# A hybrid decoder step on one core: all cache copies on the load queue, ten value slots, later splits of the output weights

## The chip, the cores and the metric

The kernel runs on one NeuronCore of a Trainium2 chip. The time is the device time of one execution in microseconds (us). The kernel before was timed in three runs: 383.45 us median, 382.65 to 383.95. One further execution was profiled; its own time was 379.59 us, with a span of 377.5 us between its first and its last instruction. PE is TensorE, DVE VectorE, ACT ScalarE, POOL GpSimd and SP SyncE.

## The reference

One layer step for a prompt of 512 tokens and a sample of 8 sequences with 8 new tokens each (64 rows), model width 1024. All values are float32.

- One input projection `w_in` (1024 x 4096) gives q, k, v and a gate for 8 attention heads of 64, and b, c, h and a gate for 512 channels of a short convolution.
- Attention: three causal branches per head, (window, dilation) = (128, 1), (512, 4), (2048, 16), merged by their softmax denominators, which is one softmax over the union of keys with each key weighted by how many branches hold it. The sample also looks at a cache of 2048 past keys and values per sequence; of these 1280 are ever looked at.
- Convolution: `u = c * h`, `y = causal 3-tap convolution of u` (with a state of two rows for the sample), `z = b * y * silu(g_conv)`.
- `mix = [attention * silu(g_att), z]`, one output projection `w_out` (1024 x 1024), then `LayerNorm(2**0.25 * x + out)` with gain and bias.
- Outputs: the new rows of x, and the new key and value caches and convolution states. The caches are returned as a whole, so the old keys and values (67 MB) are copied from inputs to outputs.

## The kernel before

**Numbers.** To keep float32 accuracy on TensorE each operand is split into a high part (a float32r cast by ScalarE) and a low part (what is left, a subtraction by VectorE), and each product is three matmuls: high by high, high by low, low by high. `x_hi`/`x_lo` hold the activations, `w_hi`/`w_lo` two weight tiles, `wo` both parts of `w_out`.

**Input projection.** `w_in` comes as 32 tiles of 128 output features (`w_tiles`, 512 KB each). A tile is loaded into one of two slots of `w_raw` (`load_w`, L227), cast (`split_hi`, L396, the cast is L402), subtracted (`split_lo`, L678, L681) and used by `project` (L1001, matmuls L997 to L999), in two halves of 288 token columns, `pj[0]` and `pj[1]`. A load of tile t waits until tile t-2 has been subtracted; a cast of tile t waits until tile t-2 has been projected.

**Rounds.** After three first tiles (v, q, k of head pair 0) the kernel runs over four head pairs: three rounds of eight tiles (`pe_round` L1156, `act_round` L556, `dve_round` L853) and a last, shorter one (`pe_last_round` L1209, `act_last_round` L605, `dve_last_round` L894). A round projects c, h, b and the convolution's gate, the next pair's v, this pair's attention gate, and the next pair's q and k, and weaves in the pair's attention for the prompt (`prompt_scores`, `prompt_turn`, `prompt_values`) and for the sample (`sample_scores` over four key pieces, `sample_turn`, `sample_values` over ten value pieces). The order on every engine is written out by hand; semaphores tie them together.

**Cache pieces.** Of each head pair's cache the used part comes as 4 key pieces (1280 KB each, one slot each in `k_buf`) and 10 value pieces (512 KB each), for which `v_buf` has 8 slots (`V_SLOTS`, L45). `load_v` (L241) waits until the piece that held its slot has been used (L1139 counts). So eight pieces of the next round can be loaded as soon as this round's are used, while pieces 8 and 9 come within their round.

**Queues.** All loads and the stores of new values are issued by SyncE, in the order of its program (L249 to L358). All copies of the caches from DRAM to DRAM, 60 of 1 MB or 1.25 MB, are issued by ScalarE: `copy_next()` (L434) stands between its other instructions, 12 times in each round. First go 24 pieces of the unused rest, then 16 of the used keys, then 20 of the used values. SyncE's program in a round:

```python
for j in range(5):
    load_w(t0 + 3 + j)
    if j:
        load_k(i + 1, j - 1)
    if i == 0 and j < 4:
        load_v(0, 2 * j); load_v(0, 2 * j + 1)
load_w(t0 + 8); load_w(t0 + 9)
load_v(i, 8); load_v(i, 9); save_v(i + 1)
load_v(i + 1, 0); load_v(i + 1, 1)
load_w(t0 + 10)
for n in range(2, 8): load_v(i + 1, n)
save_k(i + 1)
```

**Output projection.** The eight pieces of `w_out` are loaded in the last round (`load_wo`, L307), into space that the attention's buffers give free; `split_wo` (L538, cast L540) and `split_wo_lo` (L794, L797) make their two parts. TensorE multiplies five token tiles (0, 1, 2, the sample, 3; L1256 to L1300), VectorE adds the residual and does the LayerNorm (L954 to L989), SyncE loads the residual rows (`x_res`) and stores `y`. Before the first matmul (L1294) the first parts of `mix` must be split (`split_mix` L543, `split_mix_lo` L800); on VectorE that stands behind all eight `split_wo_lo`.

**Convolution and gates.** `conv_taps` (L780) makes `y_pad`, `conv_out_half` (L824) multiplies it by b into `zb`, `gate_half` (L759) makes 1 / (1 + exp(-g)) and multiplies. `out_sample` (L527) copies the sample's attention out of PSUM into `o_s`, `sample_out_turn` (L1149) transposes it at the start of the next round.

## Time and profile before

| | |
|---|---|
| three timed runs | 383.45 us median (382.65 to 383.95) |
| profiled execution, own time | 379.59 us |
| its span | 377.5 us |
| mean granted TensorE clock | 0.989 |
| PE busy | 353.8 us, 94% |
| DVE, ACT, POOL busy | 198.5 us, 117.4 us, 10.9 us |
| DMA | 141.06 MB, mean 374 GB/s |
| queue of SyncE (q1), of ScalarE (q10) | 73.46 MB, 67.11 MB |

Times are counted from the first instruction. A row of a timeline is one instruction or a run of equal ones: start, duration, engine, line, operation, tiles written and read, and in brackets how long the engine was idle before it and what ended that. SPq and ACTq are instructions that issue a DMA. A row of windows gives a stretch, its length, the busy time and count of instructions for PE, its weight loads, DVE, ACT and POOL, then the granted clock (1.00 is 2.4 GHz), the busy share of the 16 DMA engines and what they moved.

### The profile page before, as it was taken

To read this page: it belongs to the slowest core of one execution; us is meant where nothing else is said; L and a number is where in the kernel's file an instruction comes from. 1 tells how busy PE (TensorE), PEld (TensorE's weight loads), DVE (VectorE), ACT (ScalarE), POOL (GpSimd) and SP (SyncE) were. 2 spreads that over 40 slices of the span, in tenths; PEclk is the share of its full clock that TensorE was granted. 3 is DMA by queue.
4 is the path that set the end of the run, shared out by engine and by line. 5 is a ranking of instruction groups with operands and counts; after the bars stand their busy time and mean duration, and the time that the engine had idled before them with its cause. 6 is when DMAs were issued, how large, how long until landed. Compare 5 with 4: busy or idle time off the path is not lost.

```text
span 377.5 us, 7664 instructions
## 1 busy us (share of the span) xinstructions
PE 353.8 (94%) x3256; PEld 311.3 (82%) x3256; DVE 198.5 (53%) x371; ACT 117.4 (31%) x236; POOL 10.9 (3%) x28
## 2 busy tenths in 40 slices
PE   1999999997999999999999799999998998999991
PEld 1899888896988888999988689999787997888780
DVE  2533446817314368571242486711536799284765
ACT  4523423313213243431241243412525643220100
POOL 0010000000000000001000000010000002000000
PEclk9999999998999999999999999999999999999997
DMA  7999999999999999899999999999999886999931
GB/s 279 408 413 423 419 417 423 419 423 422 413 416 418 421 379 413 316 403 369 394 418 418 383 418 395 423 394 406 415 416 408 326 333 216 366 317 366 361 124 56
DMA packets 34547, 141.06 MB, mean 374 GB/s; under 512 B 3409, under 2 KB 3793, under 8 KB 32465
## 3 DMA queue, kind: packets, MB, share of 16 engines
q1 hardware_dynamic: 18194, 73.46, 48.9%
q10 hardware_dynamic: 16320, 67.11, 45.8%
q8 instruction: 26, 0.43, 0.4%
q14 instruction: 7, 0.06, 0.0%
HBM read 135.80 MB, written 71.86 MB: 550 GB/s over the span
## 4 chain that ended last, share of the span: by engine, by line
PE 62%; DMA 28%; DVE 4%; ACT 2%; SPq 2%; issue 1%; ACTq 0%
DMA w_raw<-in_w_tiles 26%; PE pj_a L997 7%; PE pj_b L997 6%; PE pj_a L999 6%; PE pj_a L998 6%; PE pj_b L998 6%; PE pj_b L999 6%; PE sc L1136 5%; PE px L1294 3%; PE px L1296 3%; PE px L1295 3%; PE sc L1100 2%; DVE w_lo L681 2%; ACT w_hi L402 2%; DMA k_buf<-in_xT 2%; PE po L1079 1%
## 5 line engine op out<-in xcount | busy, mean ns | idle before, releaser
L997 PE MATMUL pj_a<-x_hi,w_hi 128*128 128x288 f32 x256 | 79.8, 312 | 9.7 <-DVE x_lo L688 8.3
L997 PE MATMUL pj_b<-x_hi,w_hi 128*128 128x288 f32 x256 | 79.1, 309 | 0.0
L998 PE MATMUL pj_a<-x_lo,w_hi 128*128 128x288 f32 x256 | 76.5, 299 | 0.0
L999 PE MATMUL pj_a<-x_hi,w_lo 128*128 128x288 f32 x256 | 76.5, 299 | 0.0
L998 PE MATMUL pj_b<-x_lo,w_hi 128*128 128x288 f32 x256 | 76.1, 297 | 0.0
L999 PE MATMUL pj_b<-x_hi,w_lo 128*128 128x288 f32 x256 | 75.9, 297 | 0.0
L681 DVE TENSOR_TENSOR w_lo<-w_raw,w_hi 128x1024 fp32r<-128x1024 f32 x32 | 39.1, 1223 | 50.9 <-ACT w_hi L402 50.9
L997 PEld LDWEIGHTS pj_a<-x_hi,w_hi 128*128 128x128 f32 x256 | 49.2, 192 | 18.3 <-issue 9.3
L402 ACT CAST w_hi<-w_raw 128x1024 fp32r<-128x1024 f32 x32 | 33.5, 1046 | 87.3 <-DMA w_raw<-in_w_tiles 55.6
L997 PEld LDWEIGHTS pj_b<-x_hi,w_hi 128*128 128x128 f32 x256 | 48.6, 190 | 4.1 <-issue 2.6
L998 PEld LDWEIGHTS pj_a<-x_lo,w_hi 128*128 128x128 f32 x256 | 49.3, 193 | 0.0
L999 PEld LDWEIGHTS pj_a<-x_hi,w_lo 128*128 128x128 f32 x256 | 49.2, 192 | 0.0
L998 PEld LDWEIGHTS pj_b<-x_lo,w_hi 128*128 128x128 f32 x256 | 48.6, 190 | 0.0
L999 PEld LDWEIGHTS pj_b<-x_hi,w_lo 128*128 128x128 f32 x256 | 48.5, 190 | 0.0
L767 DVE RECIPROCAL rg<-rg 128x288 f32<-128x288 f32 x16 | 31.2, 1953 | 0.6
L488 ACT ACTIVATE p_pr<-p_pr,stat 128x512 f32<-128x512 f32 (+3 forms) x32 | 17.7, 555 | 27.1 <-DVE stat L732 27.1
L732 DVE CUSTOM_DVE_ANT_0 p_pr<-px,mask_pr 128x512 f32<-128x512 f32 (+3 forms) x32 | 14.4, 486 | 18.8 <-PE px L1049 18.8
L1136 PE MATMUL sc<-v_buf,pt_s 128*32 128x128 f32 x640 | 21.4, 276 | 0.0
L1100 PE MATMUL sc<-k_buf,q_bd 128*32 128x320 f32 x256 | 20.5, 438 | 0.9 <-DVE stat L754 0.9
L1294 PE MATMUL px<-wo,x_hi 128*128 128x512 f32 x48 | 19.1, 397 | 1.2 <-issue 1.2
L1296 PE MATMUL px<-wo,x_lo 128*128 128x512 f32 x48 | 19.0, 396 | 0.0
L1136 PEld LDWEIGHTS sc<-v_buf,pt_s 128*32 128x32 f32 x640 | 16.3, 109 | 3.3 <-issue 3.0
(124 smaller groups left out, 403.4 us busy)
## 6 DMA issues: line engine op xcount, KB each, us to landing
k_buf<-in_k_used SPq DMA_DIRECT2D x16, 1280.0 KB, 15.2
v_buf<-in_v_used SPq DMA_DIRECT2D x40, 512.0 KB, 18.4
out_k_used_out<-in_k_used ACTq DMA_DIRECT2D x16, 1280.0 KB, 11.6
out_v_used_out<-in_v_used ACTq DMA_DIRECT2D x20, 1024.0 KB, 10.8
w_raw<-in_w_tiles SPq DMA_DIRECT2D x32, 512.0 KB, 11.5
out_k_rest_out<-in_k_rest ACTq DMA_DIRECT2D x12, 1024.0 KB, 11.5
out_v_rest_out<-in_v_rest ACTq DMA_DIRECT2D x12, 1024.0 KB, 11.3
wo_raw<-in_w_out SPq DMA_DIRECT2D x8, 512.0 KB, 8.6
```

The costliest lines, as they stand in the source:

```text
L402: nc.scalar.copy(w_hi[:, c], w_raw[:, c]).then_inc(w_hi_done, 1)
L488: nc.scalar.activation(p, p, ACT.Exp, bias=negmax_pr[:, e:e + 1], scale=-1.0, accum_out=sum_pr[:, e:e + 1]).then_inc(pr_exp, 1)
L681: nc.vector.tensor_tensor(w_lo[:, c], w_raw[:, c], w_hi[:, c].bitcast(F32), ALU.subtract)\
L732: nc.vector.tensor_tensor_reduce(out=p_pr[:, e * SEQ:e * SEQ + w], in0=px[e][:, 0:w], in1=mask_pr[:, SEQ - w:], scale=-SCALE, scalar=BIG, ...
L767: nc.vector.reciprocal(rg[:, c], rg[:, c]).then_inc(g_step, 1)
L997: nc.tensor.matmul(out, w_hi[:, w], x_hi[:, c], start=(k == 0), stop=False)
L998: nc.tensor.matmul(out, w_hi[:, w], x_lo[:, c], start=False, stop=False)
L999: return nc.tensor.matmul(out, w_lo[:, w], x_hi[:, c], start=False, stop=(k == KT - 1))
L1100: last = nc.tensor.matmul(sc[r * 32:r * 32 + 32, 0:K_COLS], q, k_buf[:, k0:k0 + K_COLS], start=(b == 0), stop=(b == 1 and not ends), skip_ ...
L1136: last = nc.tensor.matmul(sc[r * 32:r * 32 + 32, b * P:(b + 1) * P], pt_s[:, t * P + r * 32:t * P + r * 32 + 32], v_buf[:, v0:v0 + P], sta ...
L1294: nc.tensor.matmul(out, x_hi[:, tok], wo[:, hi], start=(n == 0), stop=False)
L1296: last = nc.tensor.matmul(out, x_lo[:, tok], wo[:, hi], start=False, stop=(n == KT - 1))
```

## The change

- The copies leave ScalarE. `copy_next()` and its helpers stand in SyncE's program, on the queue of the loads; the order of the 60 copies is the same. In the loop each step is a weight tile's load, then value or key pieces, then one or two copies: 11 copies a round. Four stand in the start, eight in the last round beside the loads of `w_out`, two behind the last two weight tiles, and 13 among the loads of `x_res` and the stores of `y`.
- `V_SLOTS` is 10. The value pieces of a head pair are loaded in their own round, behind its first four weight tiles; the last round's behind its two weight tiles and between the pieces of `w_out`.
- Room for the two slots: `zb` goes, `conv_out_half` writes its product back into `y_pad`; `o_s` is now the first 256 columns of `y_pad`. So the first tap waits on `so_turned`, and the gate's multiply of the second half becomes one of 224 prompt columns and one of 64 sample columns.
- In the last round `split_wo(0)`, `(1)` and `(2)` move behind the moves of the sample's turns (`move_sample`), with the subtractions `split_wo_lo(0)` to `(2)` later too.

```diff
-V_SLOTS = 8
+V_SLOTS = V_PIECES
...
-        zb = sb("zb", [P, NT])
-        o_s = sb("o_s", [P, 2 * P], stack=early)
+        o_s = y_pad[:, 0:2 * P]
...
             load_k(0, 1)
+            copy_next()
             save_v(0)
             load_w(5)
             load_k(0, 2)
+            copy_next()
             load_k(0, 3)
+            copy_next()
+            copy_next()
             save_k(0)
             for i in range(NPAIR - 1):
                 t0 = tile0(i)
...
+                load_w(t0 + 3)
+                for n in range(0, 3):
+                    load_v(i, n)
+                copy_next()
+                load_w(t0 + 4)
+                for n in range(3, 6):
+                    load_v(i, n)
+                copy_next()
+                load_w(t0 + 5)
+                for n in range(6, 8):
+                    load_v(i, n)
+                copy_next()
+                copy_next()
+                load_w(t0 + 6)
+                for n in range(8, 10):
+                    load_v(i, n)
+                copy_next()
+                copy_next()
+                load_w(t0 + 7)
+                load_k(i + 1, 0)
+                copy_next()
+                load_w(t0 + 8)
+                load_k(i + 1, 1)
+                copy_next()
+                load_w(t0 + 9)
+                load_k(i + 1, 2)
+                copy_next()
+                save_v(i + 1)
+                load_w(t0 + 10)
+                load_k(i + 1, 3)
+                copy_next()
+                copy_next()
+                save_k(i + 1)
             load_w(W_TILES - 2)
+            for n in range(0, 2):
+                load_v(NPAIR - 1, n)
+            copy_next()
             load_w(W_TILES - 1)
+            for n in range(2, 4):
+                load_v(NPAIR - 1, n)
+            copy_next()
...
             sp.wait_ge(k_used, pieces + 1)
             load_wo(0)
+            load_v(NPAIR - 1, 4)
+            load_v(NPAIR - 1, 5)
+            copy_next()
             sp.wait_ge(k_used, pieces + 2)
             load_wo(1)
+            load_v(NPAIR - 1, 6)
+            load_v(NPAIR - 1, 7)
+            copy_next()
             sp.wait_ge(k_used, pieces + 3)
             load_wo(2)
+            load_v(NPAIR - 1, 8)
+            load_v(NPAIR - 1, 9)
+            copy_next()
+            copy_next()
             sp.wait_ge(k_used, pieces + 4)
             load_wo(3)
             load_wo(4)
+            copy_next()
...
             load_wo(5)
             load_wo(6)
+            copy_next()
+            copy_next()
             sp.wait_ge(s_masked, K_PIECES * NPAIR)
             load_wo(7)
-            load_v(NPAIR - 1, 8)
-            load_v(NPAIR - 1, 9)
+            copy_next()
...
                              d["x_rows"][y_rows(t), :]).then_inc(res_in[t % 2], 16)
+                for _ in range((0, 4, 4, 3, 2)[t]):
+                    copy_next()
...
                 exp_prompt(i, 3)
-                copy_next()
-                split_wo(0)
                 exp_sample(i)
                 move_prompt(i, 3)
                 split_hi(t0 + 4)
-                copy_next()
-                split_wo(1)
                 out_prompt(i)
                 move_sample(i, 0)
                 move_sample(i, 1)
-                split_wo(2)
+                split_wo(0)
+                split_wo(1)
                 exp_gate(t0 + G_CONV, 0)
                 move_sample(i, 2)
+                split_wo(2)
                 split_wo(3)
...
-                if gate == 0:
-                    nc.vector.tensor_tensor(rg[:, c], rg[:, c], zb[:, c], ALU.mult).then_inc(g_step, 1)
+                if gate == 0 and h == 0:
+                    nc.vector.tensor_tensor(rg[:, c], rg[:, c], y_pad[:, c], ALU.mult).then_inc(g_step, 1)
+                elif gate == 0:
+                    nc.vector.tensor_tensor(rg[:, HALF:SEQ], rg[:, HALF:SEQ], y_pad[:, HALF:SEQ], ALU.mult)\
+                        .then_inc(g_prompt, 1)
+                    r = rg[:, SEQ:].rearrange("p (b t) -> p b t", t=DEC_SEQ)
+                    nc.vector.tensor_tensor(r, r, y_s[:, :, 0:DEC_SEQ], ALU.mult).then_inc(g_step, 1)
+                    dve.wait_ge(g_prompt, i + 1)
...
                     dve.wait_ge(padded, i + 1)
+                    if i:
+                        dve.wait_ge(so_turned, i)
...
                 conv_taps(i, 1)
-                split_wo_lo(0)
                 norm_sample(i)
                 conv_taps(i, 2)
                 conv_out_half(i, 0)
                 conv_out_half(i, 1)
                 split_lo(t0 + 4)
+                split_wo_lo(0)
                 split_wo_lo(1)
-                split_wo_lo(2)
                 z_read(i)
                 gate_half(i, 0, 0)
+                split_wo_lo(2)
                 split_wo_lo(3)
                 gate_half(i, 0, 1)
```

## Rows read from the trace of the kernel before

**Rows 1.** Windows by stage: stretch, its length, each engine's busy time, clock, DMA share, GB/s.
```profile
31.30:109.10 77.80, 75.72 (x758) 67.67 (x756) 38.23 (x78) 24.02 (x50) 1.24 (x5) 0.98 1.02 419
109.10:183.40 74.30, 74.30 (x762) 66.55 (x758) 37.31 (x77) 23.74 (x52) 2.29 (x5) 1.00 0.99 391
183.40:260.00 76.60, 74.42 (x762) 66.64 (x758) 37.21 (x77) 23.79 (x52) 2.29 (x5) 1.00 1.01 405
260.00:314.90 54.90, 53.18 (x601) 46.47 (x599) 35.68 (x72) 26.09 (x53) 0.38 (x2) 1.00 0.94 370
314.90:316.70 1.80, 0.61 (x20) 0.36 (x17) 1.80 (x3) 0.37 (x1) 0.00 (x0) 1.00 0.02 5
```

**Rows 2.** Waits, whole span: total us, times, longest.
```profile
ACT w_hi L402 <- DMA w_raw<-in_w_tiles: 55.6, 12, 11.2
```

**Rows 3.** Timeline of ScalarE, three casts of weight tiles: start, us; idle time before.
```profile
83.90 1.05 ACT L402 CAST w_hi<-w_raw 128x1024 fp32r<-128x1024 f32 x1 [7.67 <-DMA w_raw<-in_w_tiles]
...
210.99 1.05 ACT L402 CAST w_hi<-w_raw 128x1024 fp32r<-128x1024 f32 x1 [11.18 <-DMA w_raw<-in_w_tiles]
...
284.48 1.04 ACT L402 CAST w_hi<-w_raw 128x1024 fp32r<-128x1024 f32 x1 [4.12 <-DMA w_raw<-in_w_tiles]
```

**Rows 4.** Timeline of SyncE's queue at the end of the second round.
```profile
175.53 0.33 SPq L231 DMA_DIRECT2D w_raw<-in_w_tiles  x1
175.90 7.43 SPq L246 DMA_DIRECT2D v_buf<-in_v_used  x6
...
185.69 1.35 SPq L231 DMA_DIRECT2D w_raw<-in_w_tiles  x1
```

**Rows 5.** DMA queue of the page: packets, MB, share of 16 engines' span.
```profile
q10 hardware_dynamic: 16320, 67.11, 45.8%
```

**Rows 6.** Windows around two stalls: before, in and behind the first, then the third round's.
```profile
82.50:85.90 3.40, 3.40 (x26) 3.17 (x24) 0.92 (x1) 2.00 (x4) 0.00 (x0) 1.00 1.01 415
85.90:89.30 3.40, 1.56 (x36) 1.09 (x35) 3.30 (x5) 1.61 (x4) 0.00 (x0) 1.00 1.01 413
89.30:92.70 3.40, 3.15 (x13) 3.18 (x14) 3.30 (x6) 0.00 (x0) 0.00 (x0) 0.51 1.04 433
...
208.00:214.60 6.60, 4.42 (x41) 3.90 (x39) 2.53 (x5) 1.80 (x3) 0.00 (x0) 1.00 0.97 382
```

**Rows 7.** DMA issues of the page: KB each, median us to landing.
```profile
k_buf<-in_k_used SPq DMA_DIRECT2D x16, 1280.0 KB, 15.2
v_buf<-in_v_used SPq DMA_DIRECT2D x40, 512.0 KB, 18.4
out_k_used_out<-in_k_used ACTq DMA_DIRECT2D x16, 1280.0 KB, 11.6
out_v_used_out<-in_v_used ACTq DMA_DIRECT2D x20, 1024.0 KB, 10.8
w_raw<-in_w_tiles SPq DMA_DIRECT2D x32, 512.0 KB, 11.5
```

**Rows 8.** Windows by what the DMA engines move.
```profile
245.00:246.50 1.50, 1.50 (x36) 1.14 (x35) 0.46 (x1) 0.40 (x1) 0.00 (x0) 1.00 0.99 410
...
330.00:337.00 7.00, 7.00 (x31) 5.63 (x31) 6.63 (x11) 2.38 (x3) 0.00 (x0) 1.00 1.03 317
...
225.00:262.00 37.00, 37.00 (x427) 34.44 (x418) 18.60 (x27) 11.29 (x21) 1.72 (x3) 1.00 1.02 405
262.00:290.00 28.00, 26.28 (x274) 21.39 (x273) 12.71 (x44) 11.92 (x30) 0.38 (x2) 1.00 1.02 414
```

**Rows 9.** Timeline of VectorE at the end of the last round.
```profile
300.67 0.30 DVE L765 TENSOR_SCALAR rg<-rg 128x288 f32<-128x288 f32 x1
...
313.66 2.35 DVE L797 TENSOR_TENSOR wo<-wo_raw,wo 128x1024 fp32r<-128x1024 f32 x2
315.93 1.29 DVE L803 TENSOR_TENSOR x_lo<-mix,x_hi 128x512 fp32r<-128x512 f32 x2
```

**Rows 10.** Timeline of VectorE: the last tile's second half.
```profile
369.46 0.69 DVE L966 SCALAR_TENSOR_TENSOR y_t<-x_res,px 128x512 f32<-128x512 f32 x1 [4.60 <-PE px L1296]
```

More of the change, by code:

```diff
@@ L256, in _, with short_runs, copy_rest, copy_k @@
             sp.dma_start(mask_s[:, :], d["mask_s"]).then_inc(small_in, 16)
+            def short_runs(rows):
+                if rows.shape[1] == K_SLOT:
+                    rows = rows.rearrange("r (m n) -> (r m) n", m=2)
+                return rows.rearrange("(r a) n -> a r n", a=16)
+            def copy_rest(n):
+                name = ("k_rest", "v_rest")[n % 2]
+                rows = slice(n // 2 * 256, (n // 2 + 1) * 256)
+                sp.dma_start(short_runs(d[name + "_out"][rows, :]), short_runs(d[name][rows, :])).then_inc(copied, 16)
+            def copy_k(i, c):
+                rows = slice((K_PIECES * i + c) * P, (K_PIECES * i + c + 1) * P)
+                sp.dma_start(short_runs(d["k_used_out"][rows, :]), short_runs(d["k_used"][rows, :]))\
+                    .then_inc(copied, 16)
+            def copy_v(i, s):
+                rows = slice((V_PIECES * i + 2 * s) * P, (V_PIECES * i + 2 * s + 2) * P)
+                sp.dma_start(short_runs(d["v_used_out"][rows, :]), short_runs(d["v_used"][rows, :]))\
+                    .then_inc(copied, 16)
+            copies = iter(range(2 * REST_ROWS + NPAIR * (K_PIECES + V_PIECES // 2)))
+            def copy_next():
+                n = next(copies)
+                if n < 2 * REST_ROWS:
+                    copy_rest(n)
+                elif n < 2 * REST_ROWS + NPAIR * K_PIECES:
+                    n -= 2 * REST_ROWS
+                    copy_k(n // K_PIECES, n % K_PIECES)
+                else:
+                    n -= 2 * REST_ROWS + NPAIR * K_PIECES
+                    copy_v(n // (V_PIECES // 2), n % (V_PIECES // 2))
             def save_v(i):
@@ L283, in _ @@
                 t0 = tile0(i)
-                for j in range(5):
-                    load_w(t0 + 3 + j)
-                    if j:
-                        load_k(i + 1, j - 1)
-                    if i == 0 and j < 4:
-                        load_v(0, 2 * j)
-                        load_v(0, 2 * j + 1)
+                load_w(t0 + 3)
[19 more added lines that the diff above has]
+                copy_next()
                 load_w(t0 + 8)
+                load_k(i + 1, 1)
+                copy_next()
                 load_w(t0 + 9)
-                load_v(i, 8)
-                load_v(i, 9)
+                load_k(i + 1, 2)
+                copy_next()
                 save_v(i + 1)
-                load_v(i + 1, 0)
-                load_v(i + 1, 1)
                 load_w(t0 + 10)
-                for n in range(2, 8):
-                    load_v(i + 1, n)
+                load_k(i + 1, 3)
+                copy_next()
+                copy_next()
                 save_k(i + 1)
             load_w(W_TILES - 2)
+            for n in range(0, 2):
+                load_v(NPAIR - 1, n)
+            copy_next()
             load_w(W_TILES - 1)
+            for n in range(2, 4):
+                load_v(NPAIR - 1, n)
+            copy_next()
             def load_wo(n):
@@ L558, in act_round @@
                 copy_c(i, 0)
-                copy_next()
                 if i:
```

63 lines of the change are left out of this document (4 added, 59 removed).

## The prediction

> **What bounds the kernel now.** I read the windows by stage first, since the page's mean mixes five stages. One round of the loop costs PE 74.3 us when nothing holds it: the second round has 74.30 us of PE work in 74.30. The first took 77.80, the third 76.60, and at the end of the last one PE idles 1.2 us of 1.80 before the output projection [rows 1]. So PE bounds the kernel, and between the start and the tail only its few stalls can be won: about 3.5 us in the first round, 2.3 in the third, and in the last 54.9 - 53.2 = 1.7 plus the 1.2.
>
> The waits say what those stalls hang on: ScalarE waited 55.6 us for weight tiles, 12 times [rows 2]. Three of these waits end where PE stalls: at 83.90, 210.99 and 284.48 [rows 3]. In order behind each such cast stand PSUM copies for which PE waits. In the first round it cost twice: PE was busy 1.56 of 3.40 us, and then the granted clock was 0.51 (1.2 GHz) for 3.4 us, with 13 matmuls where 26 ran before [rows 6].
>
> Why the tiles come late stands in SyncE's queue: six value loads go in at 175.90, and the weight tile issued at 185.69 is cast at 210.99, 25 us later [rows 3, 4]. The copies, all on ScalarE's queue, take 45.8% of the engines' time [rows 5], so the loads get about half of some 410 GB/s. DMA is nearly full as well: share 1.02, 0.99, 1.01 and 0.94 in the four rounds [rows 1].
>
> **Part 1: order of the loads, ten slots.** In MB (10^6 bytes, from the KB of [rows 7]): a weight tile 0.524, a value piece 0.524, a key piece 1.311, a copy 1.049 (1.311 for the sixteen of k_used). A round now issues 8 weight tiles 4.19, 10 values 5.24, 4 keys 5.24, small stores 0.59 and 11 copies 11.5 (14.4 if of k_used): 26.8 MB, in the third round 29.7. At 419 GB/s (first round, other copies) and 405 (k_used) [rows 1, 8] that is 64 and 73 us, both below 74.3. Each step begins with its weight tile and carries 2.9 to 4.8 MB, 7 to 12 us; so a tile has at most one step's leftover ahead of it and lands 3 to 8 us behind its issue, where ScalarE wants it some 18 behind (two projections on). The first step of round 0 is the worst: the start's four copies and four key pieces are ahead; by my sum (bytes over 420 GB/s) it lands near 47, when the cast is due. So the w_raw waits of rounds 0 and 2 go: -3.7 us (3.5 of the row, plus 0.2 for two transposes that round 0 lacks) and -2.3 = **-6.0 us**, the slow clock's loss in it. What is late next in a round is PE itself, so nothing more comes. If a round's bytes didn't fit, this would be lost (rivals C, D).
>
> **Part 2: 60 issues from ScalarE to SyncE.** No PE stall ended on one of them; I take 0 (bounds -0.3 to 0). On SyncE each stands behind its step's loads, in a queue that otherwise waits for slots; the next step's weight tile is free some 9 us later. 0.
>
> **Part 3: z in place, no zb, sample output in y_pad.** One 288-column multiply becomes two: 0.15 us more on VectorE per round (0.05 to 0.3), in the loop beside PE's work. The new wait on so_turned is for two transposes that PE did at the round's start, some 20 us before; behind it stand the taps and VectorE's whole round, but it is passed. 0.
>
> **Part 4: the splits of w_out.** At the end of the last round VectorE is the bound: from 300.67 it runs to 315.93 and half of the next 1.29 us, and PE starts the projection at 316.7 [rows 1, 9]. Of the eight splits (2.35 for two, 1.15 each by start distance) before had three done by 300.67; the new order has two, and the first now waits for a ScalarE cast behind the sample's turns. That chain gets 1.15 + 0.15 longer and starts up to 0.8 sooner against the round, as it no longer waits for w_raw: **+0.5 us** (0 to 1.3), and the stall behind 284.48 (1.1 us) brings nothing, hidden in this chain. Without another delay the projection would start at 316.7 - 6.0 + 0.5 = 311.2.
>
> **Part 5: the loads of w_out in the queue.** Here I see the largest cost. The last round used to have eight of its ten value pieces under way. Now all ten are issued in it, ahead of or between w_out's, each step with copies. Before w_out's last piece the queue moves in the last round 2 + 10 + 8 loads = 10.5 MB, 3 copies of k_used 3.9, 6 of v_used 6.3: 20.7 MB, and ahead of that the third round's 29.7. The new round starts are 31.3, 105.3, 179.6 and 253.9. At 179.6 the queue still holds the last step of the round before: 4.75 MB, issued 66.4 us into a round (175.53 - 109.1 [rows 1, 4]), 7.9 before its end; at 405 GB/s 11.7 us, with 0.9 of start: done at 184.3. Then 29.7/405 = 73.3 and 20.7/414 = 50.0 [rows 8]; one dry gap of about 1.2 (the first three steps are through near 32 us into the round, when the fourth is issued; 0 to 3), and 1.5 to land (0.8 to 2.5, an estimate): **310.3**. Behind it come a cast (1.05), the gate's exponential and the split of mix (1.0), VectorE's subtraction and PE's start (0.9): the projection starts at 313.3. That is **+2.1** on 311.2.
>
> **Part 6: the clock.** The last round's PE work ends 54.3 us into it (54.9 and the 0.5 us that run past the stretch, less the 1.1 us stall), at 308.2, so PE sits idle for some 5 us in one or two pieces. The only stall of about 2 us in the trace was followed by the slow clock, 13 matmuls where 26 fit, 1.7 us lost; the 1.2 us at 314.9 was followed by full clock [rows 1, 6]. The projection has no slack behind it: between 0 and +1.7 for one fall, +3.4 for two; I take **+1.6**.
>
> **Part 7: the tail.** 13 copies go between x_res loads and y stores in one queue. Copies alone ran at 317 GB/s there [rows 8]: 13.6 MB is 43 us, 5 MB of x_res and y another 12, against some 61 us from the first issue to the last store. The last tile's x_res then lands about when VectorE needs it (it had 4.6 us of slack before PE ended at 369.46 [rows 10]), and the last store may stand behind one other. Bounds 0 to +3; I take **+1.0**.
>
> Sum: -6.0 + 0.5 + 2.1 + 1.6 + 1.0 = -0.8. The profiled execution took 379.59 (span 377.5 and 2.1 around it); the three timed runs have a median of 383.45, 3.9 above. On that scale 383.45 - 0.8, say **382.7**.
>
> **What one queue could change.** Copies alone ran at 410 GB/s over 1.5 us and at 317 over 7 us; beside loads the total was 405 to 419 [rows 1, 8]. The Trainium skill (DMA: Bandwidth & Descriptors, Issuing engines are not separate DMA queues) says that the DMAs of all issuers run on the same 16 engines and interleave, and that several issuers save only issue time. By that one queue is as fast as two and the sum stands; by the row of 7 us runs of copies cost more, which is rival C.
>
> **Rivals.**
> A (forecast, 0.40): as above, 380.5 to 385.5; one per cent in the DMA rate moves the landing at 310.3 by 1.2 us.
> B (0.27): w_out is not late. DMA holds 420 GB/s or more (for it: 419, and 433 for 3.4 us [rows 1, 6]; against: 405 where k_used is copied) or fewer bytes are ahead. Then VectorE's chain sets the start at 311.2 to 312.2: -5.5 to -4.5, with 0 to 1.6 of clock and 0.5 of tail 378 to 381.
> C (0.26): in one queue copies don't overlap with loads. Place: w_out's landing, then the weight tiles too. The last two rounds have 24.6 MB of copies ahead of w_out's last piece; at 385 to 330 GB/s in place of about 405 they are 3 to 14 us more: 385.8 to 397, slower than before. It decides from where copies average below 390 GB/s. For it the row of 317; against it the 410 over 1.5 us, as a step holds one or two copies.
> D (0.07): the new order does not free the weight tiles: the start's leftover holds round 0's, or the last step's each round; -6.0 falls to about -3, 384 to 387.
>
> **How the numbers follow.** No change means within 0.3%, 1.15 us. A splits into 0.16 faster, 0.17 same, 0.07 slower; B is faster but for 0.01; C slower; D 0.01 same, 0.06 slower. Together faster 0.42, same 0.19, slower 0.39. The range 378.3 to 389.5 leaves out B's best end and C's worse half, under 0.2.
>
> **What would show it.** First three rounds of 74 us, and no cast in rounds 1 and 2 that waits over 1 us for w_raw; casts of w_out's later pieces (L540's) that wait for DMA; the projection's first matmul near 313, after 3 us or more of PE idle and with a stretch at half clock; windows of mixed loads and copies at 405 to 420 GB/s from one queue. If the rounds still stall on w_raw, part 1 is wrong; if windows show 385 or less with DMA share at 1, C is right; if w_out's casts don't wait, B.

## The result and the profile after

The changed kernel took 386.92 us (median of 22 runs, 381.04 to 390.59), the kernel before 382.66 us (22 runs, 380.17 to 384.01) on the same chip. The ratio is 1.0063, 95% interval 1.0035 to 1.0092: slower by 0.6%, where I had forecast 382.7 and more likely faster than slower. The time lies in the range given, the sign is wrong. All ratios leave out runs more than 1.5% above the fastest of their kernel, here 11 of the changed kernel's 22 (the profiled one among them) and none of before's; the medians of all runs stand 1.1% apart.

The profiled execution took 388.79 us (span 386.7), 1.9 above the median, as the first trace of before was 3.1 below its own. A second trace of each (x14, x15 below) stands in between: 382.25 and 384.55.

The windows of the kernel after, by stage, columns as in [rows 1]; the round starts are at 31.8, 105.8, 180.1 and 254.4:

```profile
31.80:105.80 74.00, 74.00 (x758) 66.27 (x756) 38.49 (x79) 24.09 (x50) 2.29 (x5) 1.00 1.02 410
105.80:180.10 74.30, 74.30 (x762) 66.56 (x758) 37.61 (x78) 23.72 (x52) 2.28 (x5) 1.00 0.94 369
180.10:254.40 74.30, 74.30 (x762) 66.56 (x758) 37.61 (x78) 23.72 (x52) 2.28 (x5) 1.00 1.01 393
254.40:303.70 49.30, 47.76 (x509) 41.48 (x505) 25.01 (x59) 18.69 (x44) 0.38 (x2) 1.00 1.02 408
303.70:309.40 5.70, 0.17 (x9) 0.02 (x1) 4.46 (x7) 2.30 (x3) 0.00 (x0) 0.93 1.02 406
309.40:312.80 3.40, 3.40 (x14) 3.40 (x15) 3.28 (x4) 2.34 (x3) 0.00 (x0) 0.50 1.02 371
...
317.90:322.00 4.10, 0.07 (x4) 0.00 (x0) 2.85 (x3) 3.60 (x6) 2.02 (x2) 1.00 0.60 169
322.00:325.60 3.60, 3.57 (x9) 2.82 (x10) 3.57 (x3) 0.00 (x0) 1.09 (x1) 0.53 0.94 347
...
336.70:344.40 7.70, 7.70 (x35) 6.20 (x34) 7.19 (x12) 2.55 (x4) 0.00 (x0) 1.00 0.00 0
```

The first three rounds have no idle PE left: 74.0, 74.3 and 74.3 us against 77.8, 74.3 and 76.6 [rows 1]. Up to 254.4 the changed kernel is 5.6 us ahead. All of it and 5.3 us more goes in the next 68 us: PE stands still for 5.5 us, runs at half clock (0.50, 14 matmuls in 3.4 us), stands still for 4.1 us, and runs at 0.53 again.

The waits of ScalarE (total us, times, longest) say for what; the first line answers to [rows 2]:

```profile
ACT w_hi L478 <- DMA w_raw<-in_w_tiles: 5.9, 3, 3.3
ACT wo L576 <- DMA wo_raw<-in_w_out: 17.8, 3, 8.1
```

55.6 us of waiting for weight tiles became 5.9, and 17.8 us for `w_out` came. These are the three casts, then what PE and VectorE did behind them:

```profile
303.69 1.04 ACT L576 CAST wo<-wo_raw 128x1024 fp32r<-128x1024 f32 x1 [8.12 <-DMA wo_raw<-in_w_out]
309.47 1.04 ACT L576 CAST wo<-wo_raw 128x1024 fp32r<-128x1024 f32 x1 [3.47 <-DMA wo_raw<-in_w_out]
318.07 1.04 ACT L576 CAST wo<-wo_raw 128x1024 fp32r<-128x1024 f32 x1 [6.26 <-DMA wo_raw<-in_w_out]
```
```profile
309.38 0.61 PE L1016 MATMUL pj_b<-x_hi,w_hi 128*128 128x288 f32 x1 [5.53 <-DVE mix L793]
322.03 0.60 PE L1313 MATMUL px<-wo,x_hi 128*128 128x512 f32 x1 [4.07 <-issue]
```
```profile
304.77 1.22 DVE L816 TENSOR_TENSOR wo<-wo_raw,wo 128x1024 fp32r<-128x1024 f32 x1 [5.33 <-ACT wo L576]
319.14 1.23 DVE L816 TENSOR_TENSOR wo<-wo_raw,wo 128x1024 fp32r<-128x1024 f32 x1 [3.05 <-ACT wo L576]
378.11 1.29 DVE L985 SCALAR_TENSOR_TENSOR y_t<-x_res,px 128x512 f32<-128x512 f32 x2 [5.74 <-DMA x_res<-in_x_rows]
```

Piece 3 of `w_out` came at 303.7. VectorE's subtraction for it stands ahead of its gate's work, the gate's `mix` frees the PSUM bank, and PE's last input projection waits for that: the 5.5 us. The last piece came at 318.05 and the output projection began 4.0 us later. The third row answers to [rows 10]: the last residual rows were 5.7 us late, where before VectorE had waited for PE.

The queue and the issues on the page, for [rows 5, 7], and SyncE's timeline in the tail:

```profile
q1 hardware_dynamic: 34514, 140.57, 94.2%
...
k_buf<-in_k_used SPq DMA_DIRECT2D x16, 1280.0 KB, 9.4
v_buf<-in_v_used SPq DMA_DIRECT2D x40, 512.0 KB, 12.1
...
w_raw<-in_w_tiles SPq DMA_DIRECT2D x32, 512.0 KB, 7.5
...
wo_raw<-in_w_out SPq DMA_DIRECT2D x8, 512.0 KB, 17.4
```
```profile
319.75 2.89 SPq L276 DMA_DIRECT2D out_v_used_out<-in_v_used  x4
344.46 0.35 SPq L427 DMA_DIRECT2D out_y<-y_t  x1
344.86 0.43 SPq L420 DMA_DIRECT2D x_res<-in_x_rows  x1
345.33 3.01 SPq L276 DMA_DIRECT2D out_v_used_out<-in_v_used  x4
```

Every load of the loop lands sooner than before (weight tiles 7.5 us behind their issue, 11.5 before), but `w_out` 17.4 us behind: the queue is full there. Then it has nothing: four copies are issued by 322.6, SyncE waits for the first LayerNorm until 344.46, and from 336.7 to 344.4 the DMA engines move 0 GB/s. Nine copies are still to come, seven of them ahead of the last residual rows.

### The profile page after: what moved, and what is told of

Its sections match the earlier page's. It is cut to its first block, busy times and chain, and to the rows that moved or that the text cites. A ratio compares the mean times of both kernels' runs of the same rounds, so it can differ in the third digit from the quotient of the medians.

```text
span 386.7 us, 7672 instructions
## 1 busy us (share of the span) xinstructions
PE 356.3 (92%) x3256; PEld 313.6 (81%) x3256; DVE 201.6 (52%) x375; ACT 116.8 (30%) x236; POOL 12.5 (3%) x28
## 4 chain that ended last, share of the span: by engine, by line
PE 77%; DMA 10%; SPq 5%; DVE 4%; issue 2%; ACT 1%; DVEq 0%
PE pj_b L1016 9%; PE pj_a L1016 9%; PE pj_b L1017 8%; PE pj_b L1018 8%; PE pj_a L1018 8%; PE pj_a L1017 8%; DMA wo_raw<-in_w_out 4%; PE sc L1155 4%; PE sc L1119 4%; DMA x_res<-in_x_rows 4%; PE px L1068 3%; PE po L1098 2%; PE px L1313 2%; PE px L1314 2%; PE px L1315 2%; SPq L246 2%
## 5 line engine op out<-in xcount | busy, mean ns | idle before, releaser
L1016 PE MATMUL pj_b<-x_hi,w_hi 128*128 128x288 f32 x256 | 80.3, 314 | 5.5 <-DVE mix L793 5.5
L1017 PE MATMUL pj_b<-x_lo,w_hi 128*128 128x288 f32 x256 | 77.3, 302 | 0.0
L1018 PE MATMUL pj_b<-x_hi,w_lo 128*128 128x288 f32 x256 | 77.2, 302 | 0.0
L1016 PEld LDWEIGHTS pj_a<-x_hi,w_hi 128*128 128x128 f32 x256 | 48.6, 190 | 17.4 <-issue 8.1
L1016 PEld LDWEIGHTS pj_b<-x_hi,w_hi 128*128 128x128 f32 x256 | 49.6, 194 | 9.7 <-DVE mix L793 5.8
L691 DVE TENSOR_TENSOR w_lo<-w_raw,w_hi 128x1024 fp32r<-128x1024 f32 x32 | 39.1, 1223 | 21.9 <-ACT w_hi L478 21.9
L478 ACT CAST w_hi<-w_raw 128x1024 fp32r<-128x1024 f32 x32 | 33.5, 1045 | 55.6 <-PE pj_b L1018 49.6
L1017 PEld LDWEIGHTS pj_b<-x_lo,w_hi 128*128 128x128 f32 x256 | 49.8, 194 | 0.0
L1018 PEld LDWEIGHTS pj_b<-x_hi,w_lo 128*128 128x128 f32 x256 | 49.7, 194 | 0.0
L1313 PE MATMUL px<-wo,x_hi 128*128 128x512 f32 x48 | 19.6, 409 | 4.1 <-issue 4.1
L530 ACT COPY pt_pr<-pt 128x512 f32<-128x512 f32 (+3 forms) x32 | 12.0, 430 | 28.5 <-PE pt L1085 28.5
L1314 PE MATMUL px<-wo,x_hi 128*128 128x512 f32 x48 | 19.7, 410 | 0.0
## 6 DMA issues: line engine op xcount, KB each, us to landing
wo_raw<-in_w_out SPq DMA_DIRECT2D x8, 512.0 KB, 17.4
```

The lines of the kernel that those rows point to most:

```text
L478: nc.scalar.copy(w_hi[:, c], w_raw[:, c]).then_inc(w_hi_done, 1)
L691: nc.vector.tensor_tensor(w_lo[:, c], w_raw[:, c], w_hi[:, c].bitcast(F32), ALU.subtract)\
L1016: nc.tensor.matmul(out, w_hi[:, w], x_hi[:, c], start=(k == 0), stop=False)
L1017: nc.tensor.matmul(out, w_hi[:, w], x_lo[:, c], start=False, stop=False)
L1018: return nc.tensor.matmul(out, w_lo[:, w], x_hi[:, c], start=False, stop=(k == KT - 1))
L1313: nc.tensor.matmul(out, x_hi[:, tok], wo[:, hi], start=(n == 0), stop=False)
```

## The experiments

Each was timed against the kernel before on its chip. "Landing" is that of the last piece of `w_out` to be loaded and "start" the projection's first matmul, us in the trace.

| kernel | median, us | before | ratio (95%) | landing | start | span |
|---|---|---|---|---|---|---|
| before, two traces | | | | 304.8, 309.3 | 316.7, 321.7 | 377.5, 382.5 |
| changed | 386.92 | 382.66 | 1.0063 (1.0035 to 1.0092) | 318.1 | 322.0 | 386.7 |
| x14: the same again | 384.21 | 380.18 | 1.0103 (1.0067 to 1.0140) | 315.2 | 318.3 | 380.2 |
| x1 | 381.94 | 383.59 | 0.9981 (0.9946 to 1.0016) | 311.2 | 320.4 | 381.2 |
| x2 | 386.06 | 383.59 | 1.0088 (1.0050 to 1.0126) | 296.5 | 312.2 | 383.3 |
| x3 | 387.61 | 383.59 | 1.0106 (1.0039 to 1.0173) | 317.3 | 321.3 | 387.1 |
| x4 | 384.67 | 383.59 | 1.0050 (1.0011 to 1.0089) | 314.5 | 319.2 | 383.5 |
| x5 | 385.19 | 381.39 | 1.0080 (1.0042 to 1.0117) | 308.4 | 322.0 | 384.4 |
| x6, x13 (again) | 384.23, 384.26 | 381.39, 380.18 | 1.0091 (1.0052 to 1.0130), 1.0050 (0.9995 to 1.0105) | 315.8, 317.4 | 318.9, 320.4 | 379.6, 381.1 |
| x7 | 376.64 | 381.39 | 0.9872 (0.9823 to 0.9921) | 306.7 | 312.7 | 374.7 |
| x8 | 375.52 | 381.39 | 0.9838 (0.9793 to 0.9883) | 295.8 | 312.4 | 373.1 |
| x9 | 377.62 | 383.28 | 0.9836 (0.9784 to 0.9888) | 308.5 | 314.5 | 376.8 |
| x10 | 386.12 | 383.28 | 1.0087 (1.0048 to 1.0126) | 317.2 | 321.2 | 387.0 |
| x11 | 379.48 | 383.28 | 0.9852 (0.9791 to 0.9914) | 309.5 | 316.5 | 377.7 |
| x12 | 376.25 | 380.18 | 0.9906 (0.9874 to 0.9938) | 302.1 | 311.2 | 374.3 |

My theory after the first trace: in one queue everything ahead of `w_out` delays it, so what counts is how many copies stand there. The rivals: the later splits; one queue as such, or copies next to each other; the tail.

**x1: two queues.**
```diff
-                sp.dma_start(short_runs(d["k_used_out"] ...   # copies on SyncE
+                act.dma_start(short_runs(d["k_used_out"] ...  # at before's places
```


> The changed kernel with its 60 copies back on ScalarE's queue at their old places; the new order of the loads, the ten slots, the product in place and the later splits stay. Theory 1 (place: in one queue 19 copies stand ahead of w_out's last piece and are late with it): the rounds keep 74 to 75 us, w_out's last piece lands before 306, the projection starts at 311 to 312.5, and the kernel is 4 to 6 us faster than before. Theory 2 (the later splits or the product in place cost the 5 us at the projection's start, whatever the queue): the projection starts at 316 or later and the time is that of before or up to 2 us above. Theory 3 (the weight tiles are on time only because they share a queue with the copies): with the loads on half of the engines again casts wait for weight tiles in the first and third round and the gain of 5.6 us in the rounds falls to 2 or less.

Theory 1's numbers failed: the start was at 320.4, though where the last round begins the kernel had been 4.6 us ahead of the first trace of before. With two queues too the value pieces stand among and ahead of those of `w_out`: the last came at 311.2 (304.8 and 309.3 in the traces of before), and an earlier one held ScalarE and then VectorE:

```profile
307.27 1.23 DVE L820 TENSOR_TENSOR wo<-wo_raw,wo 128x1024 fp32r<-128x1024 f32 x1 [4.97 <-ACT wo L554]
```

PE stood for 7.0 us on that wait and then ran at 0.64 of the clock over the 8.4 us up to the start. So copies in the same queue are not needed to make `w_out` late. That the values' new place does it, when the loads have half of the engines, is the likely reading, not shown alone. Still x1 is about 1% better against before than the changed kernel is. Theory 2's numbers were met (start past 316, the time of before), though by the trace PE waited for a piece of `w_out`; x5 and x10 take the splits by themselves. Theory 3 falls: the third round lost nothing, the first 1.3 us (75.3 against 77.8 in before).

**x2: all ten copies behind `w_out`.**
```diff
             load_wo(7)
-            copy_next()     # and the other nine of the last round
+            for _ in range(10):
+                copy_next()
```


> The changed kernel with the ten copies of the last round behind the last load of w_out. Theory 1: w_out's last piece lands 8 to 14 us sooner than 318.05, the projection starts at 311 to 312.5 instead of 322, without a cast that waits over 2 us for w_out. The ten copies (some 30 us of queue) then stand ahead of the residual rows: the first x_res lands near 335, and the 23 copies and 5 MB behind 300 need some 85 us, so the end is no better than 385 to 390: time given back in the tail. Rival (w_out is late for its own place behind the ten value pieces, not for the copies): the projection still starts at 318 or later.

As theory 1 said: start at 312.2, and the time given back behind it. The landing, 296.5, came even sooner than the 304 to 310 I had. The queue was not even full while `w_out` came (window), and the residual rows then came late four times, 22.4 us in all, the last at 374.7 (VectorE's row).

```profile
285.00:296.60 11.60, 11.60 (x115) 10.87 (x115) 7.95 (x11) 7.59 (x13) 0.00 (x0) 1.00 0.67 251
```
```profile
374.69 0.69 DVE L977 SCALAR_TENSOR_TENSOR y_t<-x_res,px 128x512 f32<-128x512 f32 x1 [4.26 <-DMA x_res<-in_x_rows]
```

**x3: no two copies side by side.**
```diff
-                for n in range(6, 8): load_v(i, n)
-                copy_next(); copy_next()
+                load_v(i, 6); copy_next(); load_v(i, 7); copy_next()
```


> The changed kernel with a load between any two copies of a step, in the start, the loop and the last round; the count of copies in each step stays, the tail is untouched. In the changed kernel's trace a copy lands 3.3 to 3.4 us after the copy before it and 2.6 us after a load. Theory 1 with pairs as the cause of the low rate: five pairs between 180 us and w_out's last piece at 0.8 us each, so it lands about 4 us sooner (314), the projection starts near 318, and the kernel is 3 to 4.5 us faster than the changed one, about 1 us faster than before. Rival (the longer distance is the read and write of the copies themselves, whatever stands beside them): w_out lands within 1 us of 318, and the time is that of the changed kernel.

Landing at 317.3, start at 321.3, no faster: the rival holds. The distance between two single landings was no price; the bytes of the stretch set the landing.

**x4: the old order of the loads in one queue, old slots and splits.**
```diff
-                act.dma_start(...)   # copies leave ScalarE, all else as before
+                sp.dma_start(...)    # behind the steps where the changed kernel has them
```


> The kernel before (eight slots, its own order of loads, early splits) with its 60 copies moved to SyncE's queue at the steps where the changed kernel has them. Theory 1 (what counts is how many bytes stand ahead in the one queue, not their order): the weight tile behind the six values has 5 MB ahead, 13 us, not 25, so the stalls of rounds one and three shrink to under 1 us each without the new order; w_out's last piece has only two value pieces fewer ahead (2.6 us), lands near 315 and the projection starts near 319: 384 to 387, slower than before by 1 to 4. Rival (the order of the loads makes the rounds' gain): stalls of 2 to 4 us in rounds one and three remain and the time is 388 or more. Rival (one queue costs nothing, the late splits do): 380 or less.

Theory 1's numbers hold: the stalls of rounds one and three are gone without the new order or the ten slots, the landing is at 314.5, the start at 319.2. But the start hung on another wait, the last value pieces behind `w_out`:

```profile
315.94 1.08 PE L1127 MATMUL sc<-v_buf,pt_s 128*32 128x128 f32 x16 [5.75 <-DMA v_buf<-in_v_used]
```

**x5: the later splits alone.**
```diff
-                split_wo(0)       # behind exp_prompt(i, 3)
-                split_wo(1)       # behind split_hi(t0 + 4)
-                split_wo(2)
+                split_wo(0); split_wo(1)   # behind move_sample(i, 1)
+                split_wo(2)                # behind move_sample(i, 2)
```


> The kernel before with one part of the change alone: split_wo(0) to (2) and their subtractions at the later places. My theory (part 4 of the prediction): 0 to 1.3 us slower than before, since VectorE has one subtraction more behind its gates and is the engine for which the projection waits. Rival (these splits are what made the changed kernel slow): 3 us slower or more. Rival (they wait for nothing where they stood and cost nothing where they stand): within 0.5 us of before.

0.8% slower, 3 us, where I had 0 to 1.3. That is the number of the first rival, and as much as the whole change costs (0.6 to 1.0%). What speaks against that rival is not this run but x10, where the early splits bring the changed kernel nothing, and x7, faster than before with the late ones. The term itself was 1.3: against the last input projection VectorE's chain ends 1.3 us later than in [rows 9]. But PE was then busy for only 1.15 of 3.50 us and started the projection with a part at the lower clock (0.70 over the stretch), 1.6 us more. In neither trace of before did it. The rows of x5:

```profile
318.40:321.90 3.50, 1.15 (x40) 0.68 (x28) 3.46 (x6) 1.80 (x3) 0.58 (x1) 1.00 0.24 79
322.00:325.50 3.50, 3.49 (x11) 2.78 (x12) 3.47 (x3) 0.04 (x1) 2.63 (x2) 0.70 1.02 360
```

**x6 and x13: the tail's counts.**
```diff
-                for _ in range((0, 4, 4, 3, 2)[t]):
+                for _ in range((0, 7, 3, 2, 1)[t]):
```


> The changed kernel with other counts of copies behind the loads of the residual rows: 0, 7, 3, 2, 1 instead of 0, 4, 4, 3, 2. In the changed kernel's trace the DMA engines are busy 0.22 of the time from 336 to 348 us, SyncE waiting for the first LayerNorm with no copy left to issue, and the last x_res lands 5.7 us after VectorE wants it. Theory (the copies fill the hole and are no longer ahead of the last x_res): no wait for x_res over 1 us in the last two tiles, 2 to 3 us faster than the changed kernel. Rival (the tail's bytes at 320 to 350 GB/s set the end however they are spread): within 1 us of the changed kernel, with the wait at another x_res.

> x6 once more, beside the changed kernel on the same chip. If the counts of the tail earn their 2 to 3 us in every execution, its median is 2 us or more below that of x14. If the tail's gain was that of one good execution, the two medians are within 1 us, and its second trace shows w_out or x_res later than the first.

The hole is filled (window: 335 GB/s where 73 moved in the changed kernel's trace) and in both traces 60.3 us pass from the projection's start to the last store, as in before, though VectorE still waited up to 2.5 and 2.8 us for rows. In the changed kernel's two they are 64.3 and 61.6. Of the 3.9 us more in the first, 1.5 are not the tail's: PE took them longer over the projection (53.8 against 52.3 us from its first matmul to its last), for the slow clock behind its 4.1 us of standing still. The late rows cost 2.4 and 1.2 us. The medians show none of it: x13 and x14 ran side by side, 384.26 and 384.21, while their ratios (1.0050 and 1.0103) differ by 2 us with intervals that overlap. With ten runs each over 5 to 8 us a gain of 1 us could hide, one of 3 could hardly. What the tail cost stays between 0 and some 2.4 us.

```profile
336.00:348.00 12.00, 12.00 (x53) 9.69 (x52) 9.00 (x16) 0.41 (x2) 0.00 (x0) 1.00 0.99 335
```

**x7: five copies ahead of `w_out`, the others behind.**
```diff
-   copies per place: start 4, rounds 11 11 11, last round 9 + 1 behind load_wo(7), tail 0 4 4 3 2
+   copies per place: start 5, rounds 11 12 11, last round 5 + 5 behind load_wo(7), tail 0 6 3 2 0
```


> The changed kernel with fewer copies ahead of w_out: five of the last round's ten stay between its loads, one goes to the start and one to the second round (where the queue ran dry for 3 to 8% of the time), the other eight go behind w_out's last piece and the first x_res loads (five, then 0, 6, 3, 2, 0 for the tiles instead of 0, 4, 4, 3, 2). Theory 1 (place in the one queue): w_out's last piece lands near 303, the projection starts at 312 to 313 with no wait for w_out over 1 us, the rows for the residual are in time, and the time is 8 to 10 us below the changed kernel's trace, 2 to 4 us faster than before. Rival (the DMA engines are short over the whole of the kernel, so what goes behind w_out comes back in the tail): the projection starts on time, but VectorE waits for x_res and the end is that of before or later. Rival (VectorE's chain, not w_out, now starts the projection): 314 to 316 and no better than before.

Theory 1: landing 306.7 (I had 303), start 312.7, 1.3% faster than before (I had 2 to 4 us; it is 4.9). ScalarE's longest wait for `w_out` was 3.6 us, not under 1. In the last round four copies fewer stand ahead of the last piece of `w_out`; counted from the start of the kernel it is two fewer, since two moved to the start and to the second round, where the queue had been dry at times. The rival of a DMA shortage over the whole falls; three waits for residual rows (8.5 us) cost PE nothing.

**x8: no copies.** The caches of the output are not written, and the wait for the copies at the end goes too.
```diff
             def copy_next():
+                return
```


> The changed kernel without its 60 copies: the caches in the output stay unwritten, everything else is computed. It shows what all copies cost together and where they cost it. Theory 1 (in the rounds the copies cost nothing once the weight tiles are on time; they cost at w_out and in the tail): rounds of 74 to 75 us as in the changed kernel, projection at 311 to 312.5 without a slow clock, no wait for x_res, span 372 to 375: 10 to 14 us faster than the changed kernel's trace, 5 to 8 us faster than before. Rival (the 5 us at the projection's start come from the later splits and VectorE's chain): the projection starts at 316 or later without copies too.

The start is at 312.4 and the ratio 0.984. So all the copies together, placed as in x7, cost 1.6 us of span (374.7 against 373.1, one trace each; 1.1 us by the medians). 1.3 us of the 1.6 are clock: both kernels stood still ahead of the start, x7 for 2.8 us and x8 for 2.4, and x7 alone ran slow behind it.

**x9 and x10: the early splits again,** in x7 and in the changed kernel.
```diff
+                split_wo(0)       # behind exp_prompt(i, 3); (1) and (2) likewise
-                split_wo(0); split_wo(1)   # behind move_sample(i, 1)
```


> x7 (five copies ahead of w_out, the others behind it) with the splits 0 to 2 of w_out, casts and subtractions, back at the early places of the kernel before. In x7's trace the chain of VectorE ends 1.3 us later against the last input projection than it did before, PE idles 1.6 us and then runs 1.3 us behind for a slow clock; x5 (the later splits alone) showed the same two steps, 1.3 and 1.6. Theory: with w_out on time the early places are free again, the projection starts near 311.2, without the slow clock: 2 to 3 us faster than x7. Rival (the pieces 0 to 2, landing at 279, 285 and 292 in x7, are too late for the early casts, so ScalarE waits for them and the weight tile's cast behind them is late): the same as x7 or slower.

> The changed kernel with the splits 0 to 2 back at their early places, w_out as late as it is there. Theory (w_out's last pieces, landing at 309 to 318, set the projection's start; the place of the first three splits is then hidden): the projection starts between 320 and 322, and the time is within 1.5 us of the changed kernel. Rival (late splits and late w_out add up): 2 to 3 us faster than the changed kernel, as in x5 in reverse.

x10 as expected: where `w_out` is late, the splits' place is hidden. x9 was not clearly faster than x7: its pieces came later than the early places want them, and behind one wait of 4.45 us PE stood for 1.9 us ahead of the last input projection.

```profile
300.46 1.05 ACT L576 CAST wo<-wo_raw 128x1024 fp32r<-128x1024 f32 x1 [4.45 <-DMA wo_raw<-in_w_out]
...
306.01 1.05 ACT L576 CAST wo<-wo_raw 128x1024 fp32r<-128x1024 f32 x1 [2.66 <-DMA wo_raw<-in_w_out]
```

**x11: x7's places with eight slots, the old order, the old product.**
```diff
-   copies per place in x4: start 4, rounds 11 11 11, last round 9 + 1 behind its loads, tail 0 4 4 3 2
+   as in x7: start 5, rounds 11 12 11, last round 5 + 5 behind its loads, tail 0 6 3 2 0
```


> The kernel before (eight slots, its own order of loads, early splits, product in its own buffer) with its copies in the one queue at the places of x7. Theory (x4 lost its stalls of rounds one and three with the old order of loads as well; what earns is the one queue with few copies ahead of w_out): within 1.5 us of x9, faster than x7. Rival (ten slots and the new order of loads earn something of their own once w_out is on time): 2 us or more slower than x9.

1.9 us behind x9 by the medians, 0.6 by the ratios, with intervals that overlap. The trace has a place for a loss: with one copy more in the start, PE waited for two value pieces of the first round (2.4 us together) and then ran at 0.55. x4, without that copy, has no such stall, nor has x7, with it and the new order. So the new order buys room in the queue; that it earns time by itself no run shows.

```profile
104.00:110.00 6.00, 3.63 (x53) 2.40 (x52) 1.68 (x2) 1.42 (x2) 0.00 (x0) 0.73 1.03 412
110.00:114.00 4.00, 4.00 (x20) 4.00 (x19) 0.00 (x0) 0.00 (x0) 0.00 (x0) 0.55 1.03 422
```

**x12: three copies ahead, early splits.**
```diff
-   x9: start 5, rounds 11 12 11, last round 5 + 5, tail 0 6 3 2 0
+   copies per place: start 4, rounds 11 12 11, last round 3 + 6, tail 0 6 4 2 1
```


> x9 (early splits) with only three copies between the loads of the last round, six behind w_out's last piece, then 0, 6, 4, 2, 1, and the start's count back at four. Theory: w_out's pieces 3 to 7 land 5 to 8 us sooner than in x9 (300 to 308), ScalarE waits for none of them for over 1 us, the projection starts at 311 to 311.8 with under 1.3 us of idle PE ahead of it and at full clock; span 371 to 374, 1 to 3 us faster than x9 and x7, 2% faster than before. Rival (what leaves the last round comes back in the tail): the projection starts on time and the end is no earlier than x9's, with waits for x_res of over 2 us at the last tile.

Start at 311.2, as expected; the idle time and the clock were not: PE still stood 2.0 us for VectorE's chain and then ran at 0.57. Up to the last piece of `w_out` the kernel issues five copies fewer than the changed one, and it is 0.9% faster than before, not 2.

```profile
309.20:311.20 2.00, 0.01 (x2) 0.03 (x1) 2.00 (x4) 1.32 (x2) 0.00 (x0) 1.00 1.07 338
311.20:314.40 3.20, 3.19 (x9) 2.47 (x10) 3.10 (x5) 0.00 (x0) 0.00 (x0) 0.57 0.98 347
```

Its nine runs lie within 2.5 us (before's 26 over 7.4). x7, x9 and x12 were timed on different chips and their intervals touch or overlap, so I can't order them; each is 0.9 to 1.6% faster than before.

**x14 and x15: both kernels again, for second traces.**


> The changed kernel once more: median 386 to 387.5. Its second trace shows how far the landing of w_out's last piece (318.05 in the first) and of the last x_res (378.09) move between executions; I expect 316 to 319 and 375 to 379.

> The kernel before once more, for a second trace. The first took 379.59 us with a median of 382.7 to 383.6 over all runs. If executions near the median differ from it in one place, that place is one where DMA is waited for (the stalls of the rounds, w_out, or x_res at the end), or a slow clock behind a stall; the project's start then stands at 318 to 321 instead of 316.7.

The changed kernel's median was 384.21, not 386 to 387.5, on a chip where before too is faster (380.18). Its landing was at 315.2 (I had 316 to 319), the last residual rows at 371.6 (375 to 379). Before's start was at 321.7 (I had 318 to 321), in an execution of 384.55 us that is no typical one for its chip (median 380.18). Of the 5.0 us more than in its first trace 1.4 came before the first round, and 2.5 around 290, where PE stood 2.0 us behind a late weight tile and then ran at half clock. In the first round PE waited 1.8 us for a value piece, and it had no slow clock there as the first trace had, so that round grew by only 0.4. The windows of x15 around the stall of the last round, where [rows 1] had lost 1.1 us:

```profile
286.00:290.00 4.00, 1.96 (x18) 1.60 (x18) 1.03 (x6) 1.99 (x6) 0.38 (x2) 0.94 0.94 357
290.00:293.00 3.00, 3.00 (x36) 1.33 (x35) 1.78 (x4) 1.42 (x3) 0.00 (x0) 0.52 0.95 350
```

## Why the prediction was wrong

The first trace's span is 386.7, the sum's 376.7 (377.5 - 0.8). The 10.0 us between them are 7.7 of a later landing, 1.0 from there to the start, and 1.3 behind it (3.9 where parts 6 and 7 had 2.6).

**Part 1 (-6.0): right.** 5.6 us at the last round's start (6.1 in the rounds, less a first round that began 0.5 later), and the weight tiles stayed on time in every one-queue trace with the new order. But the order was not needed for it: x4 has the old order in one queue and no stall, x1 the new order in two queues and one of 1.3 us.

**Part 5 is the step that failed: w_out's last piece at 310.3, +2.1.** It came at 318.05 and, in x14, at 315.2. The mechanism was right, its size 5 to 8 us too small, and the sign of the sum hung on it: on 311.2 its +2.1 became +10.8, and +7.1 in x14. Its three legs in the first trace are what the queue still held at the end of the second round, the third round, and the last round up to the landing:

```profile
180.00:189.30 9.30, 9.30 (x90) 8.03 (x82) 3.35 (x8) 3.63 (x10) 0.00 (x0) 1.00 1.01 379
189.30:265.90 76.60, 76.19 (x782) 68.17 (x778) 38.75 (x80) 24.80 (x55) 2.28 (x5) 1.00 1.01 395
265.90:318.00 52.10, 45.40 (x507) 39.68 (x507) 31.59 (x62) 18.62 (x38) 0.38 (x2) 0.93 1.00 396
```

The second round's last store landed at 189.3 where I had 185.8 (184.3 and 1.5 to land), since I let the queue be dry at the last step's issue and it held 3 us more: +3.5. The third round's bytes took 76.6 us, not 73.3: +3.3. The last leg 52.1, not 51.2: +0.9. Together the 7.7. The rates I had carried over (405 and 414, [rows 8]) were those of two queues, and one queue gave 395 and 396 there. A comparison of like stretches, x15 (two queues) and x14 (one):

```profile
31.00:105.00 74.00, 72.11 (x706) 64.66 (x706) 37.33 (x76) 22.87 (x49) 1.23 (x5) 1.00 1.02 419
```
```profile
31.00:105.00 74.00, 74.00 (x758) 66.27 (x757) 38.65 (x79) 24.15 (x51) 2.29 (x5) 1.00 1.02 413
```

Both have a share of 1.02. Over all traces this stretch moved 417 to 419 GB/s with two queues (four traces) and 405 to 413 with one (twelve), some 2% less, and 2% of the 280 us up to the landing is 5.6 us, by this estimate most of the 7.7.

Rival C is not out. By one of its marks, windows at 385 or less with the share at 1, it fails in the long legs. By the other, copies that average below 390, it doesn't: the two long legs took 128.7 us where the sum had 124.5, and if the 4.2 us are charged to their 24.6 MB of copies alone, these ran at 379 GB/s in place of 405 (an estimate). The measured time lies in C's range too (385.8 to 397). x1, with the same loads and the copies in a queue of their own, moved 417 and 413 GB/s (31 to 105 and 180 to 256 us) where the changed kernel moved 410 and 394, which speaks for the shared queue; but its copies also stand at other times. x3 shows only that copies side by side are not the cause. Part of the low rate may be neither: with one copy more in the second round (x7, x9, x11, x12) the third moved 400 to 405 GB/s, without it 391 to 397, so it may have been short of work at places.

The Trainium skill says that several issuers save only issue time (DMA: Bandwidth & Descriptors, Issuing engines are not separate DMA queues). By the two rows above, 419 against 413, two queues and one differ by 1.4% here: close to the rule, and enough to matter.

I also took only the last piece for harmful. Piece 3 already stopped ScalarE, VectorE and PE for 5.5 us. That cost nothing in the end, since the start waited for the last piece anyway; it came 4.0 us behind that landing where I had 3.0 (3.1 in x14).

**Part 4 (+0.5):** 1.3 by x5, and with the clock 2.8 where nothing else is late; hidden in the changed kernel (x10).

**Part 6 (+1.6):** two stretches at half clock, 2.7 us around the first stall and 1.5 at the start of the projection; the first hidden in the wait for the last piece. The term was about right for this trace; x14 paid only the hidden one. I had misread the rows for it, though: the stall of about 2 us in the first round was not the only one. In the third PE was busy for 4.42 of 6.60 us [rows 6], standing twice, 1.31 and 0.87 us, and the clock stayed at 1.00. x5 shows that the term belonged on part 4 as well.

**Part 7 (+1.0):** 2.4 us in the first trace (3.9 over before's 60.4 from start to end, less the 1.5 of clock in part 6), 1.2 in the second. I had summed the tail's bytes against its length and not asked when SyncE may issue them; the queue stood empty for 7.7 us and was then too full. By the medians its price stays open (0 to some 2 us).

**Parts 2 and 3 (0):** no stall in any trace ended on either. They were not tried alone.

**The base.** The sum was made against a trace 3.1 us below its kernel's median. What a typical execution has more no trace shows. x15, 4.4 above the median of its chip, has 2.5 us more at a weight tile in the last round and a wait for a value piece in the first, and in neither trace of the changed kernel does PE stall on either. So against such an execution the change gains more in the rounds than I had, and the medians still say it lost.

That place decided shows in x7 (late splits, as in the changed kernel): with five copies of the last round ahead of the last piece of `w_out` instead of nine it is 1.3% faster than before, not 0.6 to 1.0% slower. x12, with three ahead and the early splits, is 0.9% faster. What stays open: how much of the rate's 2% is the one queue, how much the copies or the order in it, and whether the early splits earn anything once `w_out` is on time.

## What to carry to other kernels

With everything in one queue, give each load a due time and sum the bytes ahead of it from the start: a queue that is always full moves each per cent of its rate into the landing of the last load that matters. Put what nobody waits for behind that load, and check that the issuing engine may issue it where the queue would otherwise be empty. And take a second trace before trusting a margin of 1%.

## What had not been expected

- 60 copies of 67 MB beside the loads cost 1.6 us of span (x7 against x8) with the DMA engines' share at 1.0 nearly throughout; the same copies in the changed kernel's places cost 5.5 to 12 us more (its two traces against x7's).
- In the changed kernel's trace an issue on SyncE took 2 to 3 us instead of 0.3 to 0.6 while some 18 us of transfers were outstanding, and up to 305 us nothing was issued more than 18.5 us ahead of its landing (in the tail one copy was, by 21.9).
- The length of PE's stop did not settle whether the clock fell. After 2.0 us (x12) it was 0.57 over 3.2 us, after 2.35 of 3.50 (x5) 0.70 over 3.5, each costing 1.6 us beyond the stop. But after 1.2 of 1.8 us [rows 1], after 1.95 (x6) and after 2.44 (x8) it stayed at 1.00. One stop of 1.23 us in the first round stands in both traces of before: the first trace fell to half clock behind it [rows 6], x15 did not.
